# A decoder step: x moved to the weights' queue, one wait removed, expert rows summed on TensorE

## What is computed

```python
pk = jax.nn.softmax(lk, axis=-1) * gp
h = jax.nn.silu(jnp.einsum('btd,edf->btef', u, lw['w_e_gate'])) * jnp.einsum('btd,edf->btef', u, lw['w_e_up'])
h = h * wts.astype(h.dtype)[..., None]
return jnp.einsum('btef,efd->btd', h, lw['w_e_down'])
...
ffn = hier_moe(x * (1 + scale) + shift, lw)
x = layer_norm(ALPHA * x + (1 + gate) * ffn, lw['ln2_g'], lw['ln2_b'])
```

## Time and profile before

| | |
|---|---|
| median of three runs | 1447.35 us (1445.74 to 1449.72) |
| the profiled execution | 1446.17 us |
| its span | 1444.4 us, 15359 instructions |
| TensorE matmul busy | 1323.1 us (92%), 6320 matmuls |
| VectorE, ScalarE, GpSimd busy | 537.3 us (37%), 236.5 us (16%), 154.9 us (11%) |
| chain that ended last | TensorE 85%, DMA 6%, VectorE 6%, ScalarE 1%, issue 1% |
| DMA | 207.24 MB, mean 143 GB/s |

### The profile page before, as it was taken

One profiled execution on the slowest core, in us unless ns is written; L12 is line 12 of the kernel. 1 busy time (PEld: TensorE's weight loads), 2 busy tenths in 40 slices (PEclk: granted clock), 3 DMA queues, 4 the chain that ended last, 5 costly groups with the idle time before them and its releaser, 6 DMA issues.

```text
span 1444.4 us, 15359 instructions
## 1 busy us (share of the span) xinstructions
PE 1323.1 (92%) x6320; PEld 984.7 (68%) x6320; DVE 537.3 (37%) x1018; ACT 236.5 (16%) x332; POOL 154.9 (11%) x201
## 2 busy tenths in 40 slices
PE   5999899999999999999999999999999959999920
PEld 2788688877877888888888867777668734444410
DVE  0627414563535020003554543341245363111138
ACT  1122111121111010002322222220000111111110
POOL 1000004880000000000000011101000011000042
PEclk9999999999999999999999999999999959999965
DMA  9612211110433221211101165538471535999741
GB/s 389 240 59 88 65 59 35 58 60 30 162 115 146 74 101 59 88 59 59 59 29 59 50 214 176 175 116 286 173 301 76 207 136 176 348 359 346 292 147 68
DMA packets 31556, 207.24 MB, mean 143 GB/s; under 512 B 3737, under 2 KB 4089, under 8 KB 17273
## 3 DMA queue, kind: packets, MB, share of 16 engines
q1 hardware_dynamic: 17616, 148.98, 28.1%
q0 software_dynamic: 13872, 57.30, 11.4%
HBM read 174.63 MB, written 32.00 MB: 143 GB/s over the span
## 4 chain that ended last, share of the span: by engine, by line
PE 85%; DMA 6%; DVE 6%; ACT 1%; issue 1%; POOL 0%; SPq 0%; DVEq 0%; ACTq 0%; POOLq 0%
PE PS L600 55%; PE PS L1123 6%; PE PS L1035 4%; PE PS L1141 3%; DMA proj<-in_wexp 3%; PE PS L629 2%; PE PS L716 1%; PE PS L982 1%; DMA proj<-in_wstream 1%; PE PS L920 1%; PE PS L726 1%; DMA ring<-in_wexp 1%; PE PS L755 1%; PE PS L910 1%; PE PS L1114 1%
## 5 line engine op out<-in xcount | busy, mean ns | idle before, releaser
L600 PE MATMUL PS<-uT,ring 128*128 128x272 f32 x2688 | 635.9, 395 | 6.9 <-ACT proj L1242 6.6
L600 PEld LDWEIGHTS PS<-uT,ring 128*128 128x128 f32 x2688 | 507.1, 190 | 123.5 <-issue 14.4
L600 PE MATMUL PS<-proj,ring 128*128 128x272 f32 x768 | 181.6, 394 | 0.0
L600 PEld LDWEIGHTS PS<-proj,ring 128*128 128x128 f32 x768 | 144.6, 190 | 32.4 <-issue 2.8
L1123 PE MATMUL PS<-proj,work 128*128 128x512 f32 x160 | 70.8, 595 | 2.9 <-DMA proj<-in_wexp 2.9
L1035 PE MATMUL PS<-ring,merged 128*128 128x256 f32 x256 | 59.4, 391 | 0.0
L1035 PEld LDWEIGHTS PS<-ring,merged 128*128 128x128 f32 x256 | 49.5, 196 | 8.5 <-issue 1.6
L1123 PEld LDWEIGHTS PS<-proj,work 128*128 128x128 f32 x160 | 29.6, 190 | 37.4 <-issue 36.7
L1753 DVE TENSOR_TENSOR work<-PS,tg 128x512 f32<-128x512 f32 x8 | 5.5, 692 | 121.2 <-PE PS L878 121.0
L2054 DVE TENSOR_TENSOR work<-work,PS 128x256 f32<-128x256 f32 x16 | 6.7, 421 | 110.7 <-ACT work L1445 110.7
L1123 PE MATMUL PS<-ring,work 128*128 128x512 f32 x96 | 44.2, 615 | 2.0 <-DMA ring<-in_wexp 2.0
(11 more groups left out here) (431 smaller groups left out, 1384.2 us busy)
## 6 DMA issues: line engine op xcount, KB each, us to landing
ring<-in_wstream SPq DMA_DIRECT2D x79, 1024.0 KB, 5.1
proj<-in_wexp SPq DMA_DIRECT2D x10, 3072.0 KB, 13.4
ring<-in_wexp SPq DMA_DIRECT2D x6, 3072.0 KB, 11.9
expert_rows<-proj SPq DMA_DIRECT2D x16, 512.0 KB, 12.7
proj<-in_caug POOLq DMA_DIRECT2D x10, 514.0 KB, 6.0
out_cm_s<-proj POOLq DMA_DIRECT2D x10, 514.0 KB, 4.5
proj<-in_wstream SPq DMA_DIRECT2D x4, 1024.0 KB, 16.0
expert_rows<-proj POOLq DMA_DIRECT2D x1, 4096.0 KB, 14.1
```

What stands on the lines that cost most here:

```text
L600: last = mm(acc(mi)[:, h, :], wblk(b % RING, kt, mi), rhs[:, kt, h * HALF:(h + 1) * HALF], start=kt == 0, stop=kt == KT - 1)
```

## The change

x is requested by SyncE, inside the weight stream, ahead of block 6. GpSimd waits until the fourth conditioning block (block 3) is finished before its four small loads. TensorE's wait at L691 is removed; the one behind the z blocks stays.

At the end, GpSimd only gathers. ScalarE makes ten diagonal matrices (identity times a routing weight per token; they lie where the first layer norm's gain and part of its bias were). TensorE multiplies each gathered row set by its diagonal and sums the two in PSUM, two banks per chunk, four matmuls of 512 columns. VectorE multiplies the sum by the gate rows and adds ALPHA times the residual. ScalarE takes the sum by a copy with an accumulated output, scales it to minus the mean, takes the sum of squares with that as bias, and the root. VectorE normalises as before, adding the negative mean.

```diff
@@ -252,6 +252,7 @@
         rows_p = [work[:, 5120 + i * 1024:6144 + i * 1024] for i in range(3)] + [mf[:, 0:1024]]
         rows_s = [gsf[0:32, 0:1024], pf[0:32, 15360:16384], pf[0:32, 16384:17408], mf[0:32, 1024:2048]]
         part = work[:, 1024:2048]
+        dg = gf[:, 0:1280].rearrange("p (c k t) -> p c k t", c=5, k=2)
         u2T = [pf[:, 12288 + i * 1024:13312 + i * 1024] for i in range(2)]
         oh = pf[:, 12288:13568].rearrange("p (c k s) -> p c k s", c=5, k=2)
         ids = pf[:, 13568:13568 + 10 * NB].rearrange("p (c k b) -> p c k b", c=5, k=2)
@@ -319,8 +320,8 @@
             sem(n) for n in ("xt_psum", "xt_ready", "gu_psum", "sg_ready", "h_ready", "h_psum", "hT_ready", "y_psum",
                              "y_ready"))
         back_got = [sem(f"back_got{c}") for c in range(len(CHUNKS))]
-        cmb_a, cmb_b, cmb_g, ln2_var, ln2_sd, y_done, r2_ready = (
-            sem(n) for n in ("cmb_a", "cmb_b", "cmb_g", "ln2_var", "ln2_sd", "y_done", "r2_ready"))
+        cmb_psum, cmb_g, dg_ready, first_done, ln2_sum, ln2_sd, y_done, r2_ready = (
+            sem(n) for n in ("cmb_psum", "cmb_g", "dg_ready", "first_done", "ln2_sum", "ln2_sd", "y_done", "r2_ready"))
         rows_zeroed, cT_loaded = sem("rows_zeroed"), sem("cT_loaded")
         y_out = sem("y_out")
         stored = sem("stored")
@@ -340,6 +341,8 @@
             def weight_block(b):
                 if b >= 2 * RING:
                     sp.wait_ge(group_done, GROUPS[b - RING + 1])
+                if b == RING + 2:
+                    sp.dma_start(uT[:], xT).then_inc(x_loaded, 16)
                 sp.dma_start(ring[:, b % RING, :], wstream[b]).then_inc(w_loaded[b % RING], 16)
 
             for b in range(RING, AT["ada", N_ADA_LAST]):
@@ -406,7 +409,7 @@
                 pool.dma_start(dst, src).then_inc(stored, 16)
                 n_stored[0] += 16
 
-            pool.dma_start(uT[:], xT).then_inc(x_loaded, 16)
+            pool.wait_ge(group_done, GROUPS[4])
             pool.dma_start(gs[:, 0, :], wgate).then_inc(rows_in_loaded, 16)
             pool.dma_start(seg0, segm).then_inc(rows_in_loaded, 16)
             pool.dma_start(wr[:], wrt).then_inc(rows_in_loaded, 16)
@@ -561,19 +564,9 @@
                                             bass.IndirectOffsetOnAxis(ap=ridx[0:L, 24 + 2 * c + k:25 + 2 * c + k], axis=0)
                                             ).then_inc(back_got[c], 16)
 
-            def gated(c):
-                L = CHUNKS[c][1]
-                a = BK[c][0][0:L, :]
-                pool.wait_ge(cmb_b, c + 1)
-                g_.tensor_tensor(a, a, (rows_s if c == 4 else rows_p)[3][0:L, :], ALU.mult).then_inc(cmb_g, 1)
-
             pool.wait_ge(row_used, 16)
             for c in range(5):
                 rows_back(c)
-                if c >= 2:
-                    gated(c - 2)
-            gated(3)
-            gated(4)
             pool.wait_ge(stored, n_stored[0])
 
         @block.tensor
@@ -688,7 +681,6 @@
                     mm(PS[:, 6, 0:80], cc("rep", 32), tg[0:32, 4, :], start=True, stop=True).then_inc(rep_psum, 1)
                 dense_block("xbc", i, uT)
 
-            pe.wait_ge(conv_silu, 12)
             for i in range(2, 4):
                 dense_block("z", i, uT)
             pe.wait_ge(conv_silu, 12)
@@ -1169,6 +1161,18 @@
             run_blocks(0, NE)
             with pe.If(further > 0):
                 run_blocks(NE, NB)
+
+            pe.wait_ge(dg_ready, 10)
+            for c, (t0, L) in enumerate(CHUNKS):
+                b = 2 * (c % 3)
+                pe.wait_ge(back_got[c], 32)
+                if c >= 3:
+                    pe.wait_ge(cmb_g, c - 2)
+                for n in range(2):
+                    for k in range(2):
+                        last = mm(PS[0:L, b + n, :], dg[0:L, c, k, 0:L], BK[c][k][0:L, n * 512:(n + 1) * 512],
+                                  start=k == 0, stop=k == 1)
+                last.then_inc(cmb_psum, 1)
 
         @block.scalar
         def _(act):
@@ -1457,19 +1461,18 @@
             run_blocks(0, NE)
             with act.If(further > 0):
                 run_blocks(NE, NB)
-            def weighted(c):
-                L = CHUNKS[c][1]
+            act.wait_ge(first_done, 1)
+            for c, (t0, L) in enumerate(CHUNKS):
+                for k in range(2):
+                    do(nc.scalar.activation(dg[0:L, c, k, 0:L], ident[0:L, 0:L], ACT.Copy, scale=rt[0:L, c, 61 + k:62 + k]), dg_ready)
+            for c, (t0, L) in enumerate(CHUNKS):
                 a = BK[c][0][0:L, :]
-                act.wait_ge(back_got[c], 32)
-                do(nc.scalar.activation(a, a, ACT.Copy, scale=rt[0:L, c, 61:62]), cmb_a)
-
-            weighted(0)
-            weighted(1)
-            for c in range(5):
-                if c + 2 < 5:
-                    weighted(c + 2)
-                act.wait_ge(ln2_var, c + 1)
-                deviation(c, ln2_sd)
+                act.wait_ge(ln2_sum, c + 1)
+                do(nc.scalar.activation(a, res[c][0:L, :], ACT.Copy, accum_out=stat[0:L, c, 0:1]))
+                do(nc.scalar.activation(stat[0:L, c, 12:13], stat[0:L, c, 0:1], ACT.Copy, scale=-1.0 / D))
+                do(nc.scalar.activation(a, res[c][0:L, :], ACT.Square, bias=stat[0:L, c, 12:13], accum_out=stat[0:L, c, 13:14]))
+                do(nc.scalar.activation(stat[0:L, c, 14:15], stat[0:L, c, 13:14], ACT.Sqrt, bias=cc("eps", L)[:, 0:1],
+                                        scale=1.0 / D), ln2_sd)
 
         @block.vector
         def _(dve):
@@ -1927,10 +1930,10 @@
                     do(v.bn_stats(stat[0:L, c, 6 * i:6 * i + 6], res[c][0:L, 512 * i:512 * i + 512]))
                 do(v.bn_aggr(stat[0:L, c, 12:14], stat[0:L, c, 0:12]), s)
 
-            def normed(dst, c, g, b, s):
+            def normed(dst, c, g, b, s, mean_=ALU.subtract):
 
                 L = CHUNKS[c][1]
-                do(v.scalar_tensor_tensor(dst, res[c][0:L, :], stat[0:L, c, 12:13], g[0:L, :], ALU.subtract, ALU.mult))
+                do(v.scalar_tensor_tensor(dst, res[c][0:L, :], stat[0:L, c, 12:13], g[0:L, :], mean_, ALU.mult))
                 do(v.scalar_tensor_tensor(dst, dst, stat[0:L, c, 14:15], b[0:L, :], ALU.mult, ALU.add), s)
 
 
@@ -2047,6 +2050,7 @@
                 row_pieces(n)
             for c in range(5):
                 normed(res[c][0:CHUNKS[c][1], :], c, ln1_g, ln1_b, dve_step)
+            dve.sem_inc(first_done, 1)
 
             def hidden(b, it=None):
                 i, v_ = b % NBUF, (b + 1 if it is None else it * NBUF + (b + 1))
@@ -2090,32 +2094,23 @@
             with dve.If(further > 0):
                 run_blocks(NE, NB)
 
-            def combined(c):
-                L = CHUNKS[c][1]
-                a, b = (t[0:L, :] for t in BK[c])
-                dve.wait_ge(back_got[c], 32)
-                dve.wait_ge(cmb_a, c + 1)
-                do(v.scalar_tensor_tensor(a, b, rt[0:L, c, 62:63], a, ALU.mult, ALU.add), cmb_b)
-
             def residual(c):
                 L = CHUNKS[c][1]
-                r = res[c][0:L, :]
-                dve.wait_ge(cmb_g, c + 1)
-                do(v.scalar_tensor_tensor(r, r, ALPHA, BK[c][0][0:L, :], ALU.mult, ALU.add))
-                moments(c, ln2_var)
+                r, a = res[c][0:L, :], BK[c][0][0:L, :]
+                dve.wait_ge(cmb_psum, c + 1)
+                do(v.tensor_tensor(a, banks(2 * (c % 3), 2)[0:L, :], (rows_s if c == 4 else rows_p)[3][0:L, :], ALU.mult), cmb_g)
+                do(v.scalar_tensor_tensor(r, r, ALPHA, a, ALU.mult, ALU.add), ln2_sum)
 
             def result_rows(c):
                 L = CHUNKS[c][1]
                 dve.wait_ge(ln2_sd, c + 1)
                 do(v.reciprocal(stat[0:L, c, 14:15], stat[0:L, c, 14:15]))
-                normed(res[c][0:L, :], c, ln2_g, ln2_b, y_done)
-
-            combined(0)
-            combined(1)
+                normed(res[c][0:L, :], c, ln2_g, ln2_b, y_done, ALU.add)
+
+            residual(0)
             for c in range(5):
-                residual(c)
-                if c + 2 < 5:
-                    combined(c + 2)
+                if c + 1 < 5:
+                    residual(c + 1)
                 result_rows(c)
 
 
```

## The result

The changed kernel takes **1424.37 us** (median of 4 runs, 1422.36 to 1425.67) against 1446.55 (1445.48 to 1449.72) on the same chip: a ratio of 0.9843 with an interval of [0.9827, 0.9859]. Timed once more beside two experiments, it took 1426.86 (1425.70 to 1428.89) against 1446.72; all eight runs together have a median of 1425.7. The forecast was 1422: 2.4 us too low by the first four runs, 3.7 by all eight, and inside its range.

A forecast was written before the change was run, and what follows sets the result against it. TensorE's waits were read first as the bound, then the DMA-filled start and the end behind the last expert matmul. Gains 1.5 + 8.4 + 15.0 = 24.9 us took 1446.17 to 1421.3, forecast as 1422; range 1415 to 1431.

The forecast's parts named there:

- Start, 1.5 us: First dense block: moving x to SyncE's queue lets TensorE start block 7 earlier, a gain of 0.95 to 2.05, taken as 1.5 us.
- it will start between 32.7 and 33.8, since TensorE will be waiting for it: Conditioning block 7 on TensorE: started at 34.75 before, now expected as soon as its transfer lands, 0.95 to 2.05 us earlier.
- the prediction's first paragraph: Start of the kernel: DMA engines run full at 422 GB/s, so a wait removed early can return on a later transfer.
- The cover that the prediction named for GpSimd's loads: Gate row matmuls: GpSimd's four delayed small loads land by about 33, six us before TensorE needs any at 40.82.
- Wait at L691, 8.4 us: Before the z blocks: removing TensorE's wait for ScalarE's convolution Silus gains 6.62 us idle plus 1.74 of lowered clock.
- the rival of its return: Scan: TensorE arrives earlier but waits there for something not moved, so the 8.4 us return; 1430, chance 0.05.
- End, 15.0 us: Final combination: VectorE paces chunks at 5.4 us, ScalarE needs 2.8; end at 1429.4 instead of 1444.4, bounds 11 to 17.
- first chunk ready at 1398.5: Final combination: gathers complete at 1394.94, then TensorE's four matmuls take 3.6 us at clock 0.50.
- Table loads per chunk: End: alternating Square and Sqrt costs two 1.28 us loads per chunk, making ScalarE the bound; 4.3 us lost, 1426, chance 0.10.
- The start loses: First dense block: block 7 or gate loads come up to 4 us late, turning 1.5 into -4; 1427, chance 0.08.
- Accumulating activations that are slow: ScalarE's loop at the end: accumulated sums take several cycles per element, 5.2 us each giving about 1449; chance 0.02.
- Slower than before: End: the changed kernel loses if ScalarE's sums take 4.8 us or more, 10.4 us per chunk; about 1449, chance 0.02.

## Why the prediction was right, and where its terms were off

**Start, 1.5 us: measured 0.3.** The step that failed is "it will start between 32.7 and 33.8, since TensorE will be waiting for it". TensorE waited for block 7 in neither kernel. The term left out TensorE's own 2.82 us per block, which follow the last block that came late. Before, that was block 1:

```profile
17.83 1.94 PE L629 MATMUL PS<-proj,cTs 128*32 128x256 f32 x16 [9.48 <-DMA proj<-in_wstream]
```

Six blocks on, 17.83 + 6 x 2.82 = 34.75 is the start of block 7 in the earlier trace rows. In the changed kernel the last late one is block 6. It and block 7 were issued and landed as follows (KB, us to landing; then SyncE's timeline), against the earlier trace rows:

```profile
ring<-in_wstream SPq DMA_DIRECT2D x1, 1024.0 KB, 25.7
...
ring<-in_wstream SPq DMA_DIRECT2D x1, 1024.0 KB, 27.4
...
5.89 0.51 SPq L346 DMA_DIRECT2D ring<-in_wstream  x1
...
6.45 0.45 SPq L346 DMA_DIRECT2D ring<-in_wstream  x1
```

Block 6 landed at 31.6 (30.2 before) and block 7 at 33.9 (33.8 before): x lies ahead of both, as it did in GpSimd's queue (issued at 1.28, landed 12.1 us later). So most of the wait for block 1 returned as a wait for block 6, as the prediction's first paragraph warns, and block 7 follows it at 31.62 + 2.82 = 34.44, measured 34.43. With block 6 at 30.2 TensorE would have been done with it near 33.0 and waiting for block 7, as the term says; why block 6 landed 1.4 us later stays open (with the old start put back it landed at 31.2 too, 25.7 us behind its issue at 5.54). That the bytes do matter where they are taken out of the way of all conditioning blocks, x behind block 7 shows. The 0.4 us more by which the first dense block was early in the first profile is no part of the change: the 32 gate row matmuls took 8.95, 10.33 and, with the old start, 9.18 us. The cover that the prediction named for GpSimd's loads was there, as TensorE's only wait at the gate rows is the 2.3 us for VectorE that it had before.

**Wait at L691, 8.4 us: measured 8.9.** Idle time and clock both, as worked out, and the rival of its return is refuted by putting it back. The z blocks take 29.5 us, 2.1 less than before, where 1.74 was forecast. The extra 1.66 us near 318 lie in one run of 16 pooling matmuls (3.90 us, or 5.59 where the clock falls). It can't be put down to the wait for certain: the slower run is in all three profiles with the wait, but also in two of the six without it that have the same start or nearly so, the second profile of the changed kernel among them.

**End, 15.0 us: measured 12.2.** VectorE's 5.4 per chunk was 5.35, ScalarE's 2.8 was 3.0 (1401.67 to 1404.65) and stayed under it, one table load of 1.28 with the next activation directly behind it, no stretched pass, no late gather. The step that failed is "first chunk ready at 1398.5": "four such matmuls took 3.6 us in a stretch at 0.50" read the x4 of a profile row as four calls of the program, and the row counts instructions, two to a float32 call. The first chunk took 6.3 us instead of 3.6 (eight instructions at the row's rate would be 7.2; the clock rose before the last of them). These 2.7 us are the difference between 15.0 and 12.2 but for 0.1, since two smaller errors cancel: the first pair of gathers was used 0.4 sooner behind the first gather, and the first root came 0.4 later.

**Sum.** 24.9 less 1.2 and 2.8, plus 0.5, is 21.4; the medians differ by 22.2 in the first four runs and by 19.9 in the second four. The profile's 23.8 holds 2.4 us more (0.4 at the gate rows, 1.66 and 0.34) that stand in no term of the prediction. So the forecast is close because its mechanisms hold for the two large terms; that the first four runs come within 2.4 us of it, with two terms short by 4.0, is in part luck.

**The rivals.** Table loads per chunk: one load in the whole end, so refuted. (By its own terms, 2.8 + 2 x 1.28, it would have been 5.4 us per chunk against 5.4, and not 5.5.) The start loses: it gained 0.3. Accumulating activations that are slow: they took 1.06 and 1.15 us, where the earlier trace rows have 1.01 and 1.15 for plain passes, with 0.19 behind each for reading the accumulator. Slower than before: every run of the changed kernel is faster than every run of the kernel before.

## What to carry to other kernels

When a transfer is moved in a queue, find the last block for which the consumer still waits, before and after, and add the consumer's own time for every block behind it: the late one passes its delay on, and the landing of the last block alone does not say when it is used. Convert between matmul calls of the program and instructions of the profile before a duration is multiplied by a count. Where one engine sets the pace of a loop, a removed contention is worth its time less what was put on that engine in exchange; moving the gate alone gained nothing that the medians show, and the gain came from handing work to the two engines that stood idle.

## What was not expected of the hardware

A float32 matmul call is two matmul instructions, about 0.43 us each for 512 columns at a granted clock of 1.00 (22 in 9.71 us), and twice that at 0.50. (The 32 matmuls of a dense half and the 128 of the two z blocks are instructions, the four per chunk of the combination are calls.) An accumulated sum on ScalarE took hardly more than a plain pass of the same size, 1.06 us against 1.01, and a further instruction of 0.19 us. And the granted clock does not fall at the same places in two executions of the same kernel: the sixteen pooling matmuls of the changed kernel's second profile took 5.59 us where the first took 3.90, both behind 2.0 us of idle time; the granted clock was 0.72 on average from 315 to 321 us in the second, and 1.00 from 314 to 320 in the first. Two neighbouring runs of that projection in TensorE's timeline of the second profile:

```profile
308.82 3.93 PE L747 MATMUL PS<-proj,ring 128*128 128x272 f32 x16
314.76 5.59 PE L747 MATMUL PS<-proj,ring 128*128 128x272 f32 x16 [2.01 <-ACTq L1292]
```

Sixteen matmuls of one form stand there at 3.93 and at 5.59. A difference of a few us between two single profiles should therefore be looked for in such stretches before a cause is given to it.
